# Splitting the down projection of the experts into float32r halves, and moving its eviction to ScalarE

## The reference, cut to what matters

```python
def per_sequence(args):
    xb, cb = args
    a = jnp.einsum('td,edf->tef', xb, w_eg)
    u = jnp.einsum('td,edf->tef', xb, w_eu)
    mid = jax.nn.silu(a) * u * cb[..., None]
    return jnp.einsum('tef,efd->td', mid, w_ed)
```

## Time and profile before

| | |
|---|---|
| time, median of 3 runs | 1280.9 us (1279.85 to 1282.06) |
| the profiled execution | 1280.47 us |
| its span in the trace | 1278.4 us |
| PE, DVE, ACT busy | 1178.3, 751.0, 469.2 us |
| granted TensorE clock, mean | 0.955 of full speed |
| first and last sil | 875.22 and 1264.76 us from the start of the span |

### The profile page before, as it was taken

The page is one execution under the profiler, slowest core; times in us unless marked ns, Lnnn a source line. Parts: engine busy times, 40 slices in busy tenths (PEclk is TensorE's granted clock), DMA queues, the critical chain, the costliest instruction groups (busy, mean ns, idle before and its releaser), DMA issues.

```text
span 1278.4 us, 14988 instructions
## 1 busy us (share of the span) xinstructions
PE 1178.3 (92%) x5452; PEld 896.4 (70%) x5452; DVE 751.0 (59%) x992; ACT 469.2 (37%) x635; POOL 198.9 (16%) x243
## 2 busy tenths in 40 slices
PE   5999999999968999999899899849999988989996
PEld 5988888887645667767788788746676665666664
DVE  3338999993424455444466434476776656656663
ACT  4432111113443444444232211124555544554552
POOL 4010000000142232220000000011222321222211
PEclk8999999999969999999799999958999999999999
DMA  6011111110100000001330233495999999999980
GB/s 224 1 50 50 49 49 49 49 49 17 42 0 1 1 1 1 1 1 34 131 83 17 90 113 129 169 320 179 324 339 320 304 322 316 334 333 314 308 267 8
DMA packets 101542, 172.28 MB, mean 135 GB/s; under 512 B 11727, under 2 KB 45690, under 8 KB 101498
## 3 DMA queue, kind: packets, MB, share of 16 engines
q1 hardware_dynamic: 91002, 154.86, 35.8%
q0 software_dynamic: 10432, 16.81, 5.4%
q10 hardware_dynamic: 64, 0.02, 0.0%
HBM read 165.35 MB, written 27.26 MB: 151 GB/s over the span
## 4 chain that ended last, share of the span: by engine, by line
PE 71%; DMA 12%; ACT 4%; DVE 4%; issue 4%; POOL 2%; SPq 2%; DVEq 0%; ACTq 0%; POOLq 0%
PE pb L1224 15%; PE pb L1226 15%; PE pb L1225 15%; DMA wgu_raw<-in_w_e_up 11%; PE pb L1506 7%; PE pb L1364 4%; PE pb L1341 4%; PE pb L1353 2%; PE pb L1273 2%; PE pb L1478 2%; PE pb L1283 1%; PE pb L1424 1%; ACT wgu_hi L772 1%; SPq L414 1%; SPq L418 1%
## 5 line engine op out<-in xcount | busy, mean ns | idle before, releaser
L1165 DVE TENSOR_TENSOR wgu_lo<-wgu_raw,wgu_hi 128x2048 fp32r<-128x2048 f32 x72 | 164.7, 2289 | 89.3 <-ACT wgu_hi L772 87.8
L1506 PE MATMUL pb<-wed,midT 128*128 128x512 f32 x288 | 136.5, 618 | 23.1 <-DVE midT L1200 23.0
L873 DVE SCALAR_TENSOR_TENSOR cv<-up,dwc,cv 128x1024 f32<-128x1024 f32 x120 | 154.1, 1284 | 3.7
L1224 PE MATMUL pb<-hT_hi,ws_hi 128*128 128x512 f32 x384 | 151.7, 395 | 0.0
L772 ACT ACTIVATE wgu_hi<-wgu_raw 128x2048 fp32r<-128x2048 f32 x72 | 137.1, 1909 | 38.0 <-DMA wgu_raw<-in_w_e_up 33.8
L1226 PE MATMUL pb<-hT_hi,ws_lo 128*128 128x512 f32 x384 | 149.5, 389 | 0.0
L1225 PE MATMUL pb<-hT_lo,ws_hi 128*128 128x512 f32 x384 | 149.5, 389 | 0.0
L1224 PE MATMUL pb<-wgu_hi,hgT_hi 128*128 128x512 f32 x288 | 130.0, 452 | 0.0
L1506 PEld LDWEIGHTS pb<-wed,midT 128*128 128x128 f32 x288 | 54.6, 196 | 87.2 <-issue 62.5
L1226 PE MATMUL pb<-wgu_hi,hgT_lo 128*128 128x512 f32 x288 | 113.2, 393 | 0.0
L1225 PE MATMUL pb<-wgu_lo,hgT_hi 128*128 128x512 f32 x288 | 112.5, 391 | 0.0
(11 more groups left out here) (281 smaller groups left out, 2019.9 us busy)
## 6 DMA issues: line engine op xcount, KB each, us to landing
wgu_raw<-in_w_e_gate SPq DMA_DIRECT2D x36, 1024.0 KB
wgu_raw<-in_w_e_up SPq DMA_DIRECT2D x36, 1024.0 KB
wed<-in_w_e_down SPq DMA_DIRECT2D x36, 1024.0 KB, 16.3
ws_raw<-in_w_in SPq DMA_DIRECT2D x24, 512.0 KB, 3.9
xs<-in_x SPq DMA_DIRECT2D x8, 512.0 KB, 8.4
wout<-in_w_out SPq DMA_DIRECT2D x1, 4096.0 KB, 12.9
xb<-in_x SPq DMA_DIRECT2D x8, 512.0 KB, 5.2
h_rows<-h SPq DMA_DIRECT2D x8, 512.0 KB, 2.7
```

Source lines behind the costliest of these rows:

```text
L873: i = v.scalar_tensor_tensor(out=cv[:, c, :], in0=src, scalar=w, in1=cv[:, c, :], op0=ALU.mult, op1=ALU.add)
L1165: v.tensor_tensor(wgu_lo[q % SLOTS][:, :, ks, :], wgu_raw[q % SLOTS][:, :, ks, :], wgu_hi[q % 2][:, :, ks, :].bitcast(F32), ALU.subtract). ...
L1224: t_.matmul(out, w(0), m(0), start=start, stop=False)
L1506: m = t_.matmul(pb[:, 4 + h, :], midT[:, f, :], wed[q][:, f, h * 512:(h + 1) * 512], start=(f == 0), stop=(f == 1))
```

## The change

The down matmul becomes three float32r matmuls for each of its four pieces. For this ACT writes `wed_hi` (`down_hi`, 128x2048) and DVE writes `wed_lo` in the place of the raw weights (`down_lo`, 128x2048); the transposed middle is split the same way, its high half by ACT and its low half by DVE. The whole result `yb` (128x1024) is evicted by ACT, so one semaphore `y_ok` takes the place of two. The core of the diff:

```diff
+            def down_hi(q, loads):
+                act.wait_ge(w_in1[q % SLOTS], loads)
+                a.activation(wed_hi[q % 2][:, :, :], wed[q % SLOTS][:, :, :], ACT.Copy).then_inc(wd_hi, 1)
...
             act.wait_ge(h2_ok, NTILE)
+            for i in range(2):
+                act.wait_ge(h2_out[i], 16 * NTILE // 2)
...
+            for q in range(2):
+                down_hi(q, 16)
...
                     expert_hi(q + 2, 0)
+                act.wait_ge(mt_ps, nth)
+                a.activation(midT[0][:, :, :], pb[:, 3, 0:FF].rearrange("p (f t) -> p f t", f=2), ACT.Copy).then_inc(mt_hi, 1)
+                if more:
                     gathered_hi(q, i * SLOTS + (q + 3))
                     expert_hi(q + 2, 1)
                 act.wait_ge(y_ps, nth)
                 act.wait_ge(wc_ok, nth)
-                a.activation(yb[q % 2][:, 0:512], pb[:, 4, :], ACT.Copy, scale=wcol[q % 2][:, :]).then_inc(y_a, 1)
+                a.activation(yb[q % 2][:, :], banks(4, 2), ACT.Copy, scale=wcol[q % 2][:, :]).then_inc(y_ok, 1)
+                if more:
+                    down_hi(q + 2, (i + (q + 2) // SLOTS) * 16 + 16)
...
+            def down_lo(q, count):
+                dve.wait_ge(wd_hi, count)
+                v.tensor_tensor(wed_lo[q % SLOTS][:, :, :], wed[q % SLOTS][:, :, :], wed_hi[q % 2][:, :, :].bitcast(F32), ALU.subtract).then_inc(wd_lo, 1)
...
             expert_lo(1, 1, 4)
+            down_lo(0, 1)
...
                 v.tensor_tensor(mid[:, :], sil[:, :], pb[:, GU_BANK[b], FF:2 * FF], ALU.mult).then_inc(mid_ok, 1)
+                if nxt:
+                    down_lo(q + 1, i * SLOTS + (q + 2))
                 if more:
                     expert_lo(q + 2, 0, i * (2 * SLOTS) + (2 * q + 5))
-                dve.wait_ge(mt_ps, nth)
-                v.tensor_copy(midT[:, :, :], pb[:, 3, 0:FF].rearrange("p (f t) -> p f t", f=2)).then_inc(mt_ok, 1)
+                dve.wait_ge(mt_hi, nth)
+                v.tensor_tensor(midT[1][:, :, :], pb[:, 3, 0:FF].rearrange("p (f t) -> p f t", f=2), midT[0][:, :, :].bitcast(F32), ALU.subtract).then_inc(mt_lo, 1)
...
-                dve.wait_ge(wc_ok, nth)
-                dve.wait_ge(y_ps, nth)
-                v.tensor_scalar(yb[b][:, 512:1024], pb[:, 5, :], wcol[b][:, :], None, ALU.mult).then_inc(y_d_ok, 1)
...
-                pe.wait_ge(mt_ok, nth)
-                pe.wait_ge(w_in1[q], i * 16 + 16)
-                pe.wait_ge(y_a, nth)
-                pe.wait_ge(y_d_ok, nth)
+                pe.wait_ge(mt_lo, nth)
+                pe.wait_ge(wd_lo, nth)
+                pe.wait_ge(y_ok, nth)
                 for h in range(2):
                     for f in range(2):
-                        m = t_.matmul(pb[:, 4 + h, :], midT[:, f, :], wed[q][:, f, h * 512:(h + 1) * 512], start=(f == 0), stop=(f == 1))
+                        m = three(pb[:, 4 + h, :], lambda s: midT[s][:, f, :], lambda s: (wed_lo[q] if s else wed_hi[q % 2])[:, f, h * 512:(h + 1) * 512], f == 0, f == 1)
                 m.then_inc(y_ps, 1)
```

More of the change, by code:

```diff
@@ L150, in build @@
     wed = [place(f"wed{i}", [P, 2, D], F32, o + 16 * K) for i, o in enumerate(WO)]
+    wed_lo = [place(f"wed_lo{i}", [P, 2, D], F32R, o + 16 * K) for i, o in enumerate(WO)]
+    wed_hi = [place(f"wed_hi{i}", [P, 2, D], F32R, R1 + 32 * K + 8 * K * i) for i in range(2)]
     hgT = [[place(f"hgT_{n}{i}", [P, KD, P], F32R, R1 + 48 * K + 8 * K * i + 4 * K * s) for s, n in enumerate(("hi", "lo"))] for i in range(2)]
@@ L162, in build @@
     mid = place("mid", [P, FF], F32, QDO + 9 * K)
-    midT = place("midT", [P, 2, P], F32, QDO + 10 * K)
+    midT = [place("midT_hi", [P, 2, P], F32R, QDO + 10 * K), place("midT_lo", [P, 2, P], F32R, ONO)]
     wout_hi = [place(f"wout_hi{k}", [P, D], F32R, o) for k, o in enumerate(
@@ L300, in build @@
         hg_in = [sem("hg_in0"), sem("hg_in1")]
-        hgt_ps, hgt_ok, gu_ps, sil_ok, mid_ok, mt_ps, mt_ok, y_ps, y_a, y_d_ok = [sem(n) for n in
-            ("hgT_ps", "hgT_ok", "gate_up", "silu", "mid", "midT_ps", "midT_ok", "y_ps", "y_sb_a", "y_sb_d")]
+        hgt_ps, hgt_ok, gu_ps, sil_ok, mid_ok, mt_ps, mt_hi, mt_lo, y_ps, y_ok = [sem(n) for n in
+            ("hgT_ps", "hgT_ok", "gate_up", "silu", "mid", "midT_ps", "midT_hi_ok", "midT_lo_ok", "y_ps", "y_sb")]
+        wd_hi, wd_lo = sem("wed_hi_ok"), sem("wed_lo_ok")
         y_out = [sem("y_out0"), sem("y_out1")]
@@ L540, in scatter @@
             def scatter(b, count, before):
-                pool.wait_ge(y_a, count + 1)
-                pool.sem_inc(pch, 1)
-                pool.wait_ge(y_d_ok, count + 1)
+                pool.wait_ge(y_ok, count + 1)
                 pool.sem_inc(pch, 1)
@@ L1189, in _, with dve_block @@
             expert_lo(1, 1, 4)
+            down_lo(0, 1)
             dve.wait_ge(bexp_ok, 1)
             last = dve.value_load(ntrip_i[0:1, 1:2], min_val=NE // SLOTS, max_val=MAXB // SLOTS - 1)
-            def dve_block(q, i, more):
+            def dve_block(q, i, more, nxt):
                 b, nth = q % 2, i * SLOTS + (q + 1)
@@ L1206, in dve_block @@
                 v.tensor_scalar(wcol[b][:, :], swt[:, bass.ds(i * SLOTS + q, 1)], 1.0, None, ALU.mult).then_inc(wc_ok, 1)
-                dve.wait_ge(wc_ok, nth)
-                dve.wait_ge(y_ps, nth)
-                v.tensor_scalar(yb[b][:, 512:1024], pb[:, 5, :], wcol[b][:, :], None, ALU.mult).then_inc(y_d_ok, 1)
             with dve.Fori(0, last) as i:
                 for q in range(SLOTS):
-                    dve_block(q, i, True)
+                    dve_block(q, i, True, True)
             for q in range(SLOTS):
-                dve_block(q, last, q < SLOTS - 2)
+                dve_block(q, last, q < SLOTS - 2, q < SLOTS - 1)
         @block.tensor
@@ L1465, in _ @@
             i.then_inc(swt_ps, 1)
-            pe.sem_inc(y_a, 1)
-            pe.sem_inc(y_d_ok, 1)
+            pe.sem_inc(y_ok, 1)
             def gather_T(b, gathers, evacuated):
```

## The result

| | before | after |
|---|---|---|
| median of the runs, same chip | 1281.48 us (4 runs, 1279.85 to 1285.89) | 1321.43 us (4 runs, 1319.56 to 1321.60) |
| ratio to before, 95% interval | | 1.0303 [1.0275, 1.0330] |
| profiled execution: time, span | 1280.47, 1278.4 us | 1321.32, 1319.5 us |
| first sil, sil of block 34, last sil | 875.22, 1255.60, 1264.76 | 877.73, 1296.35, 1304.20 |

A forecast was written before the change was run, and what follows sets the result against it. PE bound the kernel early (10.1 us a block), transfers later (11.67). After the change, 34 blocks of 11.97 us (407.0) plus 9.9 for table loads put the last sil 35.5 us later: 1316.5 us, range 1302 to 1328.

The forecast's parts named there:

- PE gains 0.71 us a block: Down matmuls on PE: 12 float32r take 2.72 us for 3.43 of 8 float32, 25.6 us in 36 blocks.
- DVE and ACT form one ring of 11.97 us: Each expert block: sil, mid, four large DVE steps, yb, down_hi, next sil run in series, 11.97 us.
- yb waits for wcol: ACT's yb: released by DVE's wcol, ending at 9.09 us after sil, not by the down matmul, there by 8.6.
- The table load is in the ring, +1.41: ACT's table load ahead of sil, once a loop iteration: adds 1.41 us each, 7 loads 9.9 us.
- The transfers are covered: Weight transfers: needing 95% of the time, they come in time; wgu_hi's wait nearly vanishes, DMA share about 0.95.
- Splitting the eviction would give back 15 us: yb: both halves on ACT put 0.43 us into each of 34 blocks, 15 us that two engines would avoid.
- PE closing the ring: Rival: DVE done before y_ps, so PE sets an 11.43 us block; 18 us less than forecast, 1298; 6%.
- Transfers late as well: Rival: late weight landings stop ACT ahead of expert_hi; half the earlier 33.8 us on top, 1333; 7%.
- Transfers hiding all: Rival: block under 11.67 us on average, only the last few blocks gain 0.7 us each, about 1277; 4%.
- The clock falling through every block: Rival: PE idling drops its clock to 1.2 GHz, block becomes 17.6 us, time about 1507; 2%.

The follow-up runs named there:

- float32 down matmul: The changed kernel with its down matmul done as 4 plain float32 ones of the high halves, low halves made but not used: 1331.50 us, ratio 1.0369.
- wcol early: The changed kernel with rcol and wcol moved on DVE from the end of the block to right behind midT_lo: 1308.14 us, ratio 1.0188.
- the reordered kernel: The changed kernel with down_hi(n+1) ahead of yb(n) on ACT and down_lo(n+1) behind wcol(n) on DVE: 1282.50 us, ratio 0.9991.

## Why the prediction was right, point by point

- **PE gains 0.71 us a block.** Right: the 12 down matmuls start between 919.51 and 922.13, then the next at 922.36, 2.85 us, of which 0.11 is a longer first start, against 2.72 forecast. In steps it is worth 0.68 (float32 down matmul against wcol early).
- **DVE and ACT form one ring of 11.97 us.** Right, 11.98 to 11.99, and shown by parts: down_hi 1.80 measured for 1.81 (the hundredth by chance, see above), yb 0.43 for 0.43, the down matmul 0.49 ahead of wcol for 0.54. PE stands 1.51 and 0.57 us in a block, forecast as 1.8 and 0.5. Of down_lo's 2.20 only 0.7 can be had back alone, since expert_hi stands next behind it; the forecast named that order (expert_lo's ACT half ready by 2.2) but gave down_lo no price of its own.
- **yb waits for wcol.** Right in 29 of 36 blocks; in the other 7 the down matmul is last, which the forecast had for block 34 only.
- **The table load is in the ring, +1.41.** Right: 13.40 to 13.41 in seven places. The 34 steps together were forecast at 416.9 us and took 418.6.
- **The transfers are covered.** Right: no wait of wgu_hi is left, and wed lands 6.8 us after its issue in the median and 22.5 at most, for 16.3 and 22.7. The share in a window between 908 and 1245 us is 0.81 to 0.99, about 0.95 having been forecast.
- **Splitting the eviction would give back 15 us.** Right, 15.4 measured; in the kernel before the same 0.43 us shows in a few blocks and costs nothing that its runs can tell from no change.
- **The rivals.** PE closing the ring came out only where wcol was moved or PE's matmuls were made longer. Transfers late as well: no. Transfers hiding all: its stated condition (yb not waiting for wcol, down_hi not ahead of sil) was made real by the reordered kernel: 1282.50 us, 1.6 below the kernel before on its chip, for the 3.6 of that rival. The Trainium skill (Perfetto Trace Analysis, Identifying the Most-Contended Engine) says to optimize first the engine of highest occupancy. For TensorE it goes by MFU and weight loads and not by matmul time, which the prediction left out, but with weight loads at 70% of the span against 59% for DVE PE still stands first. Putting the faster matmuls in by themselves was worth nothing (1284.22 against 1283.77), and the change that relieves PE at the price of the other two costs 3%. So a share over the whole span did not tell here what the change would do. The clock falling through every block: no, but see below.

The time came out 4.9 us above the forecast, the profiled span 5.5 us above its 1314.0. Term by term: the first sil is 2.5 us later. That is no sign of the change, for the kernels made from the one before have it anywhere from 874.65 to 879.33, and those made from the change from 875.13 to 878.86. The 34 steps are 1.7 us longer: up to 0.02 in each ordinary one, 0.2 in the first, where PE has work left in front of mid_T, and 0.9 in four blocks behind table loads, where its clock is lower. The last step is 0.15 shorter. From the last sil to the end it takes 15.3 us where 13.7 had been forecast, and this is the lower clock again, but not by the change: the forecast took over the tail of the one profile of the kernel before, and that is the only one of all thirteen profiles in which the clock stays at 1.00 there. In the kernel before without its scatter the same eight float32 down matmuls take 5.40 us for 3.70 (start, duration, instruction, idle before it; first the kernel before, then the one without scatter):

```profile
1266.60 3.70 PE L1506 MATMUL pb<-wed,midT 128*128 128x512 f32 x8 [0.52 <-DVE midT L1200]
```

```profile
1239.73 5.40 PE L1504 MATMUL pb<-wed,midT 128*128 128x512 f32 x8 [0.52 <-DVE midT L1198]
```

So of the 5.5 us about 4 are differences between executions, which the forecast had no means to see, and the mis-sized term proper is 1.7 us in 34 steps, half of it the clock, which was put as all or nothing and came in four blocks.

## What to carry to other kernels

Before work is given to an engine with room by its share, walk its program order: what it costs is decided by whether it stands between a wait and the instruction that another engine waits for. The same 1.8 us split cost 1.8 us a block behind yb, and fell into an existing wait when it stood ahead of yb. When such a ring is opened, look for the next bound before counting the gain: here the transfers took all of it, and only lighter transfers brought the 17.5 us to light.

## What the hardware showed that was not expected

The granted clock of TensorE drops after some gaps and not after others. While ACT loaded its table, PE stood for 2.95 us in the changed kernel. PE around that gap (start, duration, instruction):

```profile
924.86 0.39 PE L1244 MATMUL pb<-wgu_hi,hgT_lo 128*128 128x512 f32 x1
928.19 0.44 PE L1512 MATMUL pb<-ident,mid 128*128 128x128 f32 x2 [2.95 <-DVE mid L1215]
928.49 1.91 PE L1495 MATMUL pb<-ident,hg 128*128 128x128 f32 x8
...
930.62 0.63 PE L1243 MATMUL pb<-wgu_lo,hgT_hi 128*128 128x512 f32 x1
931.05 0.63 PE L1244 MATMUL pb<-wgu_hi,hgT_lo 128*128 128x512 f32 x1
...
932.46 0.40 PE L1242 MATMUL pb<-wgu_hi,hgT_hi 128*128 128x512 f32 x1
932.69 0.40 PE L1243 MATMUL pb<-wgu_lo,hgT_hi 128*128 128x512 f32 x1
```

and the windows of this place and of the next load, one iteration on:

```profile
926.00:931.00 5.00, 2.81 (x12) 2.60 (x13) 3.29 (x3) 4.31 (x5) 0.84 (x1) 0.77 1.01 338
931.00:936.00 5.00, 5.00 (x21) 4.04 (x20) 5.00 (x5) 2.26 (x2) 1.04 (x1) 0.89 0.75 224
...
976.00:981.00 5.00, 3.14 (x19) 2.80 (x20) 3.62 (x3) 4.99 (x6) 0.80 (x1) 1.00 0.95 322
```

Matmuls that start 0.23 us apart at the 2.4 GHz level start 0.43 apart here, the 1.2 GHz level, until about 932, and then 0.23 again. At the next load PE stood for 2.94 us, and the clock stayed at 1.00. In the changed kernel it is every second load after which the block is longer. The ordinary gaps of 1.5 and 0.6 us in each block had no such effect. The Trainium skill (TensorE: Matmul & The Clock Gate) says that the engine falls back to 1.2 GHz when it stands idle; the trace agrees for part of the long gaps. The price in a block is 0.2 to 0.3 us, because PE has 0.5 us in hand ahead of wcol; with float32 down matmuls, where it has none, it is 0.7. Nor is it the length of the gap alone: with wcol made early PE stood for only 2.44 us at each load, and the clock fell at six of the seven. With yb split between the engines PE stood for 2.47 to 2.52 us at each, and the clock stayed at 1.00 at the first four and fell at the last three (0.72 to 0.74 over 6 us), though the steps do not show it (11.57 or 11.58 each time). At the end the last matmuls of the changed kernel run so as well, and there nothing covers them:

```profile
1309.56 0.63 PE L1242 MATMUL pb<-wed_hi,midT_hi 128*128 128x512 f32 x1
1309.99 0.63 PE L1243 MATMUL pb<-wed_lo,midT_hi 128*128 128x512 f32 x1
```

Here it costs about 1.6 us. All eleven kernels of the experiments run their last down matmuls at a granted clock of 0.60 to 0.79 over 8 us, those made from the kernel before too, and only the profile of the kernel before has 1.00, behind the same gaps of 1.51 and 0.52 us as the one without its scatter. Why one gap of 2.95 us brings the lower clock and the next of 2.94 does not stays open: no run here varied the gap by itself.
